# A two-layer decoder step with mixture of experts: row loads of the expert tiles in SyncE's queue, a first tile gathered by matmuls, a residual summed in PSUM, and loads that start at other times

## The reference

```python
def pool_mix(ctx, start_pos, w_pool, pool_scale):
    ...
    pooled = pooled.reshape(B, n, N_POOL_GROUPS, POOL_GROUP_WIDTH)
    y = jnp.einsum('bsgc,gcd->bsgd', pooled, w_pool).reshape(B, n, D)
    return y * pool_scale

def moe(x, w_router, router_bias, w_gate, w_up, w_down):
    ...
    combine = route(t, w_router, router_bias).astype(x.dtype)
    h = jax.nn.silu(jnp.einsum('td,edf->tef', t, w_gate)) * jnp.einsum('td,edf->tef', t, w_up)
    y = jnp.einsum('tef,efd->td', h * combine[:, :, None], w_down)

    # per layer i
    xp = layer_norm(ALPHA * xp + mix_p, ln1_g[i], ln1_b[i])
    xp = layer_norm(ALPHA * xp + moe(xp, ...), ln2_g[i], ln2_b[i])
```

## Time and profile before

| what | value |
|---|---|
| median of 3 runs | 1120.07 us (1118.42 to 1121.95) |
| the profiled execution, its own time | 1120.17 us |
| its span, first to last instruction | 1118.5 us |
| mean granted clock | 0.944 |
| PE busy | 991.1 us, 89% |
| DVE, ACT, POOL busy | 382.0, 196.0, 94.9 us |
| DMA | 297.21 MB, mean 266 GB/s |

### The profile page before, as it was taken

The page is one execution under the profiler, slowest core; times in us unless marked ns, Lnnn a source line. Parts: engine busy times, 40 slices in busy tenths (PEclk is TensorE's granted clock), DMA queues, the critical chain, the costliest instruction groups (busy, mean ns, idle before and its releaser), DMA issues.

```text
span 1118.5 us, 36110 instructions
## 1 busy us (share of the span) xinstructions
PE 991.1 (89%) x15859; PEld 846.7 (76%) x15859; DVE 382.0 (34%) x861; ACT 196.0 (18%) x444; POOL 94.9 (8%) x179
## 2 busy tenths in 40 slices
PE   7979999989999597899999995972589999999975
PEld 6757777744566497899999994762589999999962
DVE  1234444423366622121221213895112122122127
ACT  1234444430042120000000010121200100000010
POOL 0011121241000210000000002002100000000011
PEclk9999999989999698999999998985799999999998
DMA  9512342714205899999999995762599999999935
GB/s 335 195 55 90 107 156 89 247 39 135 89 21 187 328 407 353 401 366 400 385 384 371 383 374 171 277 269 82 190 340 380 391 391 375 381 380 386 399 121 198
DMA packets 80477, 297.21 MB, mean 266 GB/s; under 512 B 10216, under 2 KB 40304, under 8 KB 72095
## 3 DMA queue, kind: packets, MB, share of 16 engines
q1 hardware_dynamic: 54327, 248.91, 60.0%
q10 hardware_dynamic: 17952, 25.24, 6.7%
q0 software_dynamic: 8144, 22.29, 5.7%
HBM read 255.91 MB, written 40.97 MB: 265 GB/s over the span
## 4 chain that ended last, share of the span: by engine, by line
PE 78%; DVE 9%; DMA 6%; issue 3%; POOL 2%; ACT 1%; SPq 1%; ACTq 0%; POOLq 0%; DVEq 0%
PE PS L989 16%; PE PS L1012 15%; PE PS L1001 15%; PE PS L886 5%; PE PS L639 4%; PE PS L686 3%; PE PS L974 3%; PE PS L702 3%; DMA arena<-expert_rows 2%; PE PS L595 2%; PE PS L695 2%; PE PS L617 2%; POOL expert_rows L1162 1%; PE PS L659 1%; PE PS L789 1%
## 5 line engine op out<-in xcount | busy, mean ns | idle before, releaser
L989 PE MATMUL PS<-arena,ring 128*64 128x96 f32 (+1 forms) x4096 | 188.2, 251 | 32.0 <-DVE arena L1882 30.8
L989 PEld LDWEIGHTS PS<-arena,ring 128*64 128x64 f32 x4096 | 178.2, 140 | 38.5 <-issue 38.5
L1012 PE MATMUL PS<-arena,ring 128*64 128x96 f32 (+1 forms) x4096 | 177.2, 247 | 7.3 <-DVE arena L1918 4.1
L1012 PEld LDWEIGHTS PS<-arena,ring 128*64 128x64 f32 x4096 | 172.4, 137 | 9.2 <-DVE arena L1918 5.1
L1001 PE MATMUL PS<-arena,ring 128*64 128x96 f32 (+1 forms) x4096 | 176.3, 246 | 2.9 <-issue 2.9
L1001 PEld LDWEIGHTS PS<-arena,ring 128*64 128x64 f32 x4096 | 172.2, 137 | 3.4 <-issue 3.4
L1882 DVE STREAM_TRANSPOSE arena<-arena 128x768 uint32<-128x768 uint32 x34 | 54.2, 1595 | 151.5 <-ACT arena L1372 125.7
L1926 DVE COPY arena<-PS 128x384 f32<-128x384 f32 x32 | 17.8, 557 | 160.0 <-PE PS L1012 160.0
L1383 ACT ACTIVATE arena<-PS 128x384 f32<-128x384 f32 x32 | 15.7, 490 | 255.2 <-PE PS L1012 255.2
L886 PE MATMUL PS<-ring,arena 128*128 128x512 f32 x128 | 57.0, 606 | 0.7 <-issue 0.7
L886 PEld LDWEIGHTS PS<-ring,arena 128*128 128x128 f32 x128 | 24.7, 195 | 31.0 <-issue 31.0
(11 more groups left out here) (293 smaller groups left out, 1066.1 us busy)
## 6 DMA issues: line engine op xcount, KB each, us to landing
ring<-w_up SPq DMA_DIRECT2D x32, 2048.0 KB, 17.6
ring<-w_down SPq DMA_DIRECT2D x32, 2048.0 KB, 19.9
ring<-w_gate SPq DMA_DIRECT2D x32, 2048.0 KB, 16.3
expert_out<-arena ACTq DMA_DIRECT2D x32, 384.0 KB, 12.4
arena<-expert_rows ACTq DMA_DIRECT2D x128, 96.0 KB, 9.3
expert_rows<-ring SPq DMA_DIRECT2D x6, 1920.0 KB, 9.8
ring<-cache_ckv SPq DMA_DIRECT2D x56, 128.0 KB, 2.2
expert_out<-ring SPq DMA_DIRECT2D x1, 4608.0 KB, 26.2
```

Of the source, the lines that this page charges most:

```text
L989: last = nc.tensor.matmul(bank(s, KF, n)[at:at + 64, f, :], wg[w][:, k, P * f + at:P * f + at + 64], x[:, k, :], start=(k == 0), stop=(k = ...
L1012: last = nc.tensor.matmul(bank(4 + m // 4, 4, n)[at:at + 64, m % 4, :], wd[w][:, f, P * m + at:P * m + at + 64], hh[:, f, :], start=(f == ...
```

## The change

Five things, all in one diff. SP starts w_down of expert 1 right behind w_down of expert 0. W_pool and the gains of layer 1 wait for the last tile's gate phase. In both loops SP loads each tile's rows itself, between two weight transfers; ScalarE loads only tile 1's of layer 1. No rows are loaded beyond the last tile; semaphores are counted up in their place. In layer 1 ALPHA * x enters the mixer's PSUM by a matmul with ALPHA times the identity (`alpha_id`), and statistics and first scaling read PSUM. Layer 1's tile 0 does not come from DRAM: VectorE compares each row's slot with 1 to 96 (`pick_rows`), TensorE multiplies X by these one-hot matrices, and two copies put the result into `xeT[0]`. The constants get the row 1 to 96 for it, loaded between the layers. Several waits are counted anew to match.

```diff
...
@@ -506,6 +511,8 @@
                     first_weights(wu, "w_up", 0, 1, q["wu_ld"])
                     sp.wait_ge(pv_ps, 4)
                     first_weights(wd, "w_down", 0, 1, q["wd_ld"])
+                    sp.wait_ge(sc_ps, BATCHES)
+                    first_weights(wd, "w_down", 1, 0, q["wd_ld"])
                     sp.wait_ge(pv_ps, 5)
                     first_weights(wg, "w_gate", 0, 1, q["wg_ld"])
                     sp.wait_ge(scat, 128)
@@ -514,11 +521,11 @@
                     sp.wait_ge(mix_ps, NT)
                     first_weights(wg, "w_gate", 1, 0, q["wg_ld"])
                     first_weights(wu, "w_up", 1, 0, q["wu_ld"])
-                    first_weights(wd, "w_down", 1, 0, q["wd_ld"])
                 else:
                     sp.wait_ge(S[0]["xeT_set"], 2 * nh + 1)
-                    sp.wait_ge(S[0]["xe_ld"][1], 64 * (nh + 1))
+                    sp.wait_ge(S[0]["xe_ld"][1], 64 * nh)
                     sp.dma_start(pscale, bcast(t["pool_scale"][0])).then_inc(st_ld, 16)
+                    sp.dma_start(slot_no, t["consts"][:, held:held + CAP]).then_inc(st_ld, 16)
                     sp.dma_start(state[0:DB * CTX, :], t["state_pool"][0].rearrange("b c d -> (b c) d")).then_inc(st_ld, 16)
 
                     for slot, rows in ((0, 64), (1, 64), (2, 32)):
@@ -532,6 +539,10 @@
                     load_expert(1, 1, 0, (S[0]["gate_ps"][1], nh), (S[0]["up_ps"][1], 2 * nh), (S[0]["down_ps"][1], 2 * nh))
                 sp.wait_ge(tab_set, 2 * L + 2)
                 nh = sp.value_load(n_half[0:1, 0:1], min_val=E // 2, max_val=TILES // 2)
+                def next_rows(u, s):
+                    sp.wait_ge(q["xeT_set"], 2 * u + s - 1)
+                    load_rows(sp, L, s, bass.ds(CAP * (2 * u + s), CAP))
+
                 def next_expert(u, s):
                     ex = sp.value_load(tile_ids[0:1, bass.ds(2 * u + s, 1)], min_val=0, max_val=E - 1)
                     load_expert(L, ex, 1 - s, (q["gate_ps"][s], u), (q["up_ps"][s], 2 * u), (q["down_ps"][s], 2 * u))
@@ -543,9 +554,14 @@
                     load_rows(sp, 0, 0, slice(2 * CAP, 3 * CAP))
                     load_rows(sp, 0, 1, slice(3 * CAP, 4 * CAP))
                     next_expert(1, 1)
+                else:
+                    sp.wait_ge(scat, 320)
                 with sp.Fori(2 if L == 0 else 1, nh) as u:
                     for s in range(2):
+                        next_rows(u, s)
                         next_expert(u, s)
+                sp.wait_ge(q["xe_ld"][0], 64 * nh)
+                sp.sem_inc(q["xe_ld"][0], 64)
             sp.wait_ge(ln_out[1], NT + 1)
             sp.dma_start(t["o_y_s"][:, 0, :], X[0:DB, 4, :]).then_inc(out_st, 16)
             for i in range(4):
@@ -888,9 +904,11 @@
                 else:
                     for g in range(4):
                         for kk in range(2):
-                            last = nc.tensor.matmul(view(PS, 512 * b0 + 256 * g, 256)[0:n, :],
-                                                    poolT[:, 2 * g + kk, P * i:P * i + n], wpool[:, 2 * g + kk, :],
-                                                    start=(kk == 0), stop=(kk == 1))
+                            nc.tensor.matmul(view(PS, 512 * b0 + 256 * g, 256)[0:n, :],
+                                             poolT[:, 2 * g + kk, P * i:P * i + n], wpool[:, 2 * g + kk, :],
+                                             start=(kk == 0), stop=False)
+                        last = nc.tensor.matmul(view(PS, 512 * b0 + 256 * g, 256), alpha_id, X[:, i, 256 * g:256 * (g + 1)],
+                                                start=False, stop=True)
                 last.then_inc(mix_ps, 1)
 
             def pool(i):
...
@@ -1107,6 +1125,14 @@
             for i in range(1, NT):
                 router(1, i)
             counts(3, 0, NT)
+            pe.wait_ge(picked_set, 1)
+            for k in range(KD):
+                for i in range(NT):
+                    n = rows_of(i)
+                    last = nc.tensor.matmul(bank(k // 4, 4, CAP)[:, k % 4, :],
+                                            X[0:n, i, :].rearrange("b (p k) -> b k p", k=KD)[:, k, :], picked[0:n, i, :],
+                                            start=(i == 0), stop=(i == NT - 1))
+            last.then_inc(first_ps, 1)
             experts(1)
             pe.wait_ge(xscaled, 2 * NT)
             pe.wait_ge(diag_set, 2)
@@ -1177,17 +1203,13 @@
                 for i in range(NT) if L else (NT - 1,):
                     scatter(i)
                 hold(pool_e, scat, 160 * (L + 1))
+                hold(pool_e, tab_set, 2 * L + 2)
+                nh = pool_e.value_load(n_half[0:1, 0:1], min_val=E // 2, max_val=TILES // 2)
                 if L == 0:
-                    hold(pool_e, uv_ps, 1)
+                    hold(pool_e, q["gate_ps"][1], nh)
                     pool_e.dma_start(wpool, t["w_pool"][0].rearrange("g (k p) d -> p (g k) d", p=P)).then_inc(wp_ld, 16)
-                if L == 0:
-
-                    hold(pool_e, q["xeT_set"], 1)
                     pool_e.dma_start(gb[:, 0, :], bcast(t["ln1_g"][1])).then_inc(gb_ld[1][0], 16)
                     pool_e.dma_start(gb[:, 1, :], bcast(t["ln1_b"][1])).then_inc(gb_ld[1][0], 16)
-
-                hold(pool_e, tab_set, 2 * L + 2)
-                nh = pool_e.value_load(n_half[0:1, 0:1], min_val=E // 2, max_val=TILES // 2)
                 for s in range(2):
                     hold(pool_e, q["y_st"][s], 16 * nh + 16)
                 if L == 0:
...
@@ -1346,8 +1368,9 @@
                     act.sem_inc(q["y_st"][s], 16)
 
                 if L:
+                    act.wait_ge(first_ps, 1)
                     act.wait_ge(scat, 320)
-                    load_rows(act, L, 0, slice(0, CAP))
+                    act.sem_inc(q["xe_ld"][0], 64)
                     load_rows(act, L, 1, slice(CAP, 2 * CAP))
                     for i in range(NT):
                         scale_rows(i)
@@ -1363,9 +1386,6 @@
                 def tile(u, s, more, n=CAP):
                     tl = 2 * u + s
 
-                    if n == CAP:
-                        act.wait_ge(q["xeT_set"], tl + 1)
-                        load_rows(act, L, s, bass.ds(CAP * (tl + 2), CAP))
                     if more:
                         store(tl - 1, 1 - s, 16 * (u + s))
                     act.wait_ge(q["gate_ps"][s], u + 1)
@@ -1667,6 +1687,12 @@
                 x = X[0:n, i, :]
                 if which == 0:
                     dve.wait_ge(mix_ps, NT * L + i + 1)
+                    if L and i < NT - 1:
+                        for c in range(2):
+                            ins = v.bn_stats(bn[:, i, 6 * c:6 * c + 6], bank(2 * (i % 2) + c))
+                        link(ins)
+                        v.bn_aggr(mv[:, i, :], bn[:, i, :]).then_inc(ln_agg, 1)
+                        return
                     if i < NT - 1:
                         v.scalar_tensor_tensor(out=x, in0=x, scalar=ALPHA, in1=view(PS, 1024 * (i % 2), D)[0:n, :],
                                                op0=ALU.mult, op1=ALU.add).then_inc(ln_z[L], 1)
@@ -1708,7 +1734,14 @@
                     dve.wait_ge(gb_ld[L][which], 32)
                 dve.wait_ge(ln_agg, 2 * NT * L + k)
                 z = view(PS, 1024 * (i - 1), D) if which == 1 and i in (1, 2) else x
-                link(v.scalar_tensor_tensor(out=x, in0=z, scalar=mv[0:n, i, 0:1], in1=gains, op0=ALU.subtract, op1=ALU.mult))
+                if L and which == 0 and i < NT - 1:
+                    z = view(PS, 1024 * (i % 2), D)
+                ins = v.scalar_tensor_tensor(out=x, in0=z, scalar=mv[0:n, i, 0:1], in1=gains, op0=ALU.subtract, op1=ALU.mult)
+                if L and which == 0 and i < NT - 1:
+                    ins.then_inc(ln_z[1], 1)
+                    dve.wait_ge(ln_z[1], i + 1)
+                else:
+                    link(ins)
                 dve.wait_ge(ln_std, 2 * NT * L + k)
                 link(v.reciprocal(rstd[0:n, i:i + 1], std[0:n, i:i + 1]))
                 v.scalar_tensor_tensor(out=x, in0=x, scalar=rstd[0:n, i:i + 1], in1=offsets, op0=ALU.mult, op1=ALU.add
@@ -1871,6 +1904,13 @@
                 link(v.tensor_reduce(r_nov[one, :], r_nh[one, 0:NOV // 2], AXX, ALU.add))
                 v.tensor_scalar(n_half[one, :], r_nov[one, :], float(E // 2), None, ALU.add).then_inc(tab_set, 1)
 
+            def pick_rows():
+
+                for i in range(NT):
+                    n = rows_of(i)
+                    ins = v.tensor_scalar(picked[0:n, i, :], slot_no[0:n, :], r_slot[0:n, E * i:E * i + 1], None, ALU.is_equal)
+                ins.then_inc(picked_set, 1)
+
             def experts(L):
                 q = S[L]
                 dve.wait_ge(tab_set, 2 * L + 2)
@@ -1883,10 +1923,15 @@
                                 xe[s].rearrange("p a (i m) -> p a m i", i=32).bitcast(mybir.dt.uint32)
                                 ).then_inc(q["xeT_set"], 1)
 
-                dve.wait_ge(q["xe_ld"][0], 64)
```

(9 more changed lines are left out.)

18 lines of the change are left out of this document (12 added, 6 removed).

## The result

The changed kernel is **slower**: 1142.19 us, median of 4 runs (1134.22 to 1143.9), against 1121.01 for the kernel before on the same chip (4 runs, 1118.42 to 1122.19). The ratio is 1.0174, its 95% interval 1.0146 to 1.0202. The profiled execution took 1143.9 us, its span is 1142.2. The forecast was 1107, with 1098 to 1115.5 around it.

The account below looks back on a forecast made before the run. TensorE was taken to set the pace in both expert loops, only just, with DMA engines full at 383 GB/s. A +5.5, B -6.7, C -3.1, D +0.3, E -9.0, F 0 sum to -13.0: 1107 us, range 1098 to 1115.5.

Parts of the forecast that it names:

- F: Both loops' row loads in SP's queue, behind w_down and ahead of w_gate: 0 us, between -2 and +4.
- Rival 3: Rows wait behind w_down in each late tile of either loop: +27, 1134 us; chance 0.09, shared with any other slowing.
- E: Layer 1's first tile, built by one-hot matmuls in 7 to 10 us: -9.0 us; gain 3 if slow.
- Rival 2: One-hot matmuls slow (E -3) or mixes at the lower clock (D +3): 1113 or 1110, both 1116 us; chance 0.17.
- A: Layer 0's first tile: expert 1's earlier w_down stands ahead of the scatters, +5.5 us; 0 if they pass it.
- B: Layer 0's wait before tile 2: less queued, so rows arrive in time, -6.7 us; 0 if they still come late.
- C: End of layer 0's expert loop: w_down never late, unused row loads gone, -3.1 us; at worst 0.
- D: Between the layers: norms shorten as the sum moves to TensorE, but VectorE waits for the mixer; +0.3 us, -2 to +3.

Follow-up runs that it names:

- e10: Changed kernel with a tile's rows as one transfer of 384 pieces of 1 KB to all partitions, in SyncE's queue: ratio 0.9983 to the kernel before.
- e15: e1 with e10's form of the row load, one transfer per tile, in ScalarE's queue: 1115.43 us, ratio 0.9963 to the kernel before.
- e16: Changed kernel with each of a tile's four row transfers going into every fourth partition instead of 32 neighbours: 1116.85 us, ratio 0.9970 to the kernel before.
- e1: Changed kernel with F alone undone, the loops' row loads in ScalarE's queue again: 1121.3 us, ratio 1.0004 to the kernel before.
- e2: Kernel before with F alone, the loops' row loads in SyncE's queue: 1142.76 us, ratio 1.0223 to the kernel before.
- e9: e1 with E undone too, layer 1's tile 0 loaded from scattered rows and transposed: 1114.95 us, ratio 0.9943 to the kernel before.
- e12: e9 with A undone too, w_down of expert 1 issued behind that expert's w_up again: ratio 0.9958 to the kernel before.
- e19: e9 with A and D undone too, leaving essentially the late w_pool and gains: 1114.67 us, ratio 0.9947 to the kernel before.
- e11: Changed kernel with a tile's rows as four transfers of 32 pieces of 3 KB, each into 32 neighbouring partitions: ratio 1.0074 to the kernel before.
- e18: e9 with each tile's four narrow row transfers split, two from ScalarE's queue and two from SyncE's: ratio 1.0088 to the kernel before.
- e4: Changed kernel with w_down read as 128 pieces of 16 KB instead of 512 of 4 KB: ratio 1.0113 to the kernel before.
- e8: e1 with the one-hot matmuls reading weight columns side by side instead of every eighth: 1117.74 us, ratio 0.9967 to the kernel before.
- e7: e1 with the 40 one-hot matmuls cut into 80 of half the width, 64 weight columns: 1164.16 us, ratio 1.0366 to the kernel before.

## Why the prediction was wrong, by its steps

- **F failed**, and decides. "**0**, between -2 and +4": 19 to 25 us. Three sentences of it fell. "SP's own time [...] hides" priced an issue by the 1.1 us of the earlier trace rows; in a deep queue single issues took 3.6 to 6.7 us. "In layer 0 only the last w_down comes near that": it assumed that the queue falls 1.5 us per tile behind as before; four of layer 0's last tiles were late. And the 1.5 itself was taken for the limit of the machine ("the DMA engines are full"), when 416 GB/s and more were moved at the same share of 1.02 (e10, e15, e16). The rule of the page "DMA: Bandwidth & Descriptors", section "Issuing engines are not separate DMA queues", in the Trainium skill, by which the prediction made the move worth 0, is contradicted by e1 and e2 for this kernel (issue time, which that section calls usually small beside the transfer, grew to 8 us for four transfers), and agrees with e10 against e15 (0.9983 and 0.9963, intervals overlapping), where the transfers are spread.
- **Rival 3** had the mechanism, late rows in each late tile, and a price of +27 for it, near what F cost. Its objection, "a full queue doesn't run dry when TensorE is late, so the delay doesn't add up", was wrong: the delay did add up, tile by tile. 0.09 was too little for it.
- **E failed** in the price of the matmuls: "7 to 10 us", bound 19; they took 23.0, above the bound. It counted 0.24 us once for each of the 40, as the transposes of the earlier trace rows have it. But a transpose leaves one record in the trace and a float32 matmul two: 80 records of 0.29 us. (In the same way the 128 and 16 "matmuls" in the words on the kernel before are records, of 64 and 8 matmuls.) And the full clock, which its lower figure counted on, and the start "on a warm TensorE" didn't come: 0.50 from 784 to 808, and the first tile's 32 records took 2.83 us as before. So +6.8 in place of -9.0. Rival 2 had the sign of the error, not its size.
- **A** was right where it looked (+5.1 at the last scatter, after the drift; 5.5 forecast), but some 2 of it are hidden behind VectorE, and it took nothing off tile 2's wait: from tile 0 to tile 2 it is 44.6 us with it (e9), 43.8 without (e12).
- **B and C** were right in sign, and the late w_pool and gains alone are worth 5.9 us (e19), of 9.8 forecast with A's part of B and the dropped row loads. The wait ahead of tile 2's transposes went from 5.46 to 0.75 us, as B said; the end of layer 0's loop has no late w_down in e1, e9 and e19. In the changed kernel C's gain was lost again to F.
- **D** was right in its reason, the fourth norm's wait for the mixer, and so in being small: +0.3 forecast, -2.2 to -0.3 in the traces, which the runs don't resolve. Its count, 20 records for the mix of tile 3, should have been 24; they took 5.3 us at the full clock, within its 4.6 to 8.0.
- A to D, -4.0 by the forecast, gave -6.4 (e9). A to E, -13.0, gave nothing (e1). All together: -6.4 + 6.8 + 19 = +19, the measured 1.74%; this closes by itself, since the 6.8 and the 19 are differences of the same runs.

## What to carry to other kernels

A DMA share of 1.02 says that the engines are busy, not that they can't move more: divide the bytes of a loop's turn by its time and look in slices for holes in the rate before the machine's limit is put into a sum. Many pieces into few neighbouring partitions made such holes here; give a transfer targets over all partitions where the layout allows, or keep the narrow ones in a queue in which nothing waits for them. And a matmul form that no row shows is priced by records: count how many one matmul of its kind leaves, take the time of one of the same width at the clock that is granted there, and don't borrow either from a transpose.

## What the chip showed that I had not expected

- The same four transfers of 96 pieces of 1 KB: 367 to 386 GB/s into 32 neighbouring partitions each, 418 to 419 into every fourth partition (e16). Larger pieces help the narrow form only in part (e11, 382 to 401). The Trainium skill's page "SBUF — State Buffer", section "Door 1: The DMA port swizzle", has a rule that I had not weighed: the partitions that a transfer covers decide how many of 16 ports it reaches, and by its table 32 neighbours reach 8 of them, every fourth partition all 16. The order of the two rates fits it. Its section "Can I just issue two DMAs to hit both halves?" says that two transfers don't join their ports and only one over all 128 partitions reaches all; e18 agrees with the first (365 and 390 GB/s); e16, with 32 partitions to a transfer and 418 to 419 GB/s, speaks against the second. That the ports are the cause no run shows by itself.
- SyncE's own DMA issues block for up to 6.7 us once the queue is some 25 us deep, and with narrow transfers in it. In the late tiles of the kernel before w_down was 30.7 us under way, and no issue of SyncE took over 1 us. What is full then was not settled: w_down in a quarter of the pieces freed the weights' issues, not the rows' (e4).
- Weight loads of float32, one record each, two per matmul. At a granted clock of 0.50: 0.25 us for 128 columns read at every eighth word, 0.23 side by side (e8), 0.08 for 64 columns at every eighth (e7) and 0.08 side by side. At 1.00: 0.12 for 128 and 0.04 for 64, side by side.
- 23 us of the one-hot matmuls, with TensorE busy 23.03 us of 24, all passed at a granted clock of 0.50 (784 to 808).
- 40 more matmuls ahead of a loop cost the loop 11.4 us of TensorE's time in every second turn of two tiles, without any data that was late (e7). The same code 40 matmuls shorter has none of it.
